# Swapping the halves of the rotated queries: a DMA from SBUF to SBUF in place of a permutation matmul

## The reference

```
q = rope((h @ w_q + b_q).reshape(bsz, s, N_Q_HEADS, HEAD_DIM), pos)
...
sc = jnp.einsum('bnqkgd,bnskd->bnkgqs', q, k_band,
                preferred_element_type=jnp.float32) * (HEAD_DIM ** -0.5)
```

```
t1, t2 = tf[..., :half], tf[..., half:]
out = jnp.concatenate([t1 * cos - t2 * sin, t2 * cos + t1 * sin], axis=-1)
```

## Time and profile before

| | us |
|---|---|
| median of 3 runs | 1259.94 |
| lowest and highest | 1259.32, 1260.23 |
| the profiled execution, its own time | 1257.77 |
| the profiled execution, span | 1256.0 |
| PE busy | 1228.9 (98% of the span) |
| DVE busy | 310.2 (25%) |
| ACT busy | 200.7 (16%) |
| POOL busy | 45.1 (4%) |
| granted TensorE clock, mean | 0.996 of full speed |

### The profile page before, as it was taken

How to read it: one execution, slowest core, us unless ns; L and a number is a source line. 1 busy time by engine, 2 the same in 40 slices (tenths; PEclk the granted TensorE clock), 3 DMA queues, 4 the chain that set the end, 5 groups by cost and what they waited for, 6 DMA issues and landing times.

```text
span 1256.0 us, 29092 instructions
## 1 busy us (share of the span) xinstructions
PE 1228.9 (98%) x13809; PEld 676.1 (54%) x13809; DVE 310.2 (25%) x408; ACT 200.7 (16%) x279; POOL 45.1 (4%) x41
## 2 busy tenths in 40 slices
PE   7999999989999999999999999999999999999996
PEld 6888888879743363355336335533633553363343
DVE  4554545468450101011010101101010110001002
ACT  4444443465420000000000000000000000000001
POOL 3000000011010000000000000000000000000000
PEclk9999999999999999999999999999999999999998
DMA  9965655323489999999999999999999999999960
GB/s 345 391 241 183 200 174 196 134 67 124 157 325 386 402 415 402 396 412 406 405 400 416 398 400 411 411 401 396 411 407 397 412 412 399 399 414 403 386 263 36
DMA packets 97757, 418.72 MB, mean 333 GB/s; under 512 B 8545, under 2 KB 14738, under 8 KB 97634
## 3 DMA queue, kind: packets, MB, share of 16 engines
q1 hardware_dynamic: 94288, 410.59, 83.6%
q0 software_dynamic: 1664, 5.05, 1.4%
q10 hardware_dynamic: 1682, 1.17, 0.3%
HBM read 414.68 MB, written 2.10 MB: 332 GB/s over the span
## 4 chain that ended last, share of the span: by engine, by line
PE 97%; DVE 2%; ACT 1%; DMA 0%; issue 0%; ACTq 0%; DVEq 0%
PE psum L706 46%; PE psum L717 23%; PE psum L618 8%; PE psum L620 7%; PE psum L619 7%; PE psum L697 1%; PE psum L626 1%; PE psum L687 0%; DMA consts<-in_table 0%; PE psum L873 0%; PE psum L792 0%; PE psum L896 0%; DVE x_res L1446 0%; PE psum L883 0%; PE psum L994 0%
## 5 line engine op out<-in xcount | busy, mean ns | idle before, releaser
L706 PE MATMUL psum<-up,xg 128*32 128x448 f32 x6144 | 580.4, 539 | 0.6 <-DVE xg L1670 0.6
L706 PEld LDWEIGHTS psum<-up,xg 128*32 128x32 f32 x6144 | 198.8, 110 | 373.3 <-issue 370.1
L717 PE MATMUL psum<-down,hid_t 128*32 128x256 f32 x5376 | 291.5, 379 | 0.0
L717 PEld LDWEIGHTS psum<-down,hid_t 128*32 128x32 f32 x5376 | 174.7, 110 | 117.9 <-issue 3.9
L1419 DVE TENSOR_TENSOR sil<-sil,psum 128x1344 f32<-128x1344 f32 x16 | 24.9, 1554 | 463.9 <-PE psum L706 463.9
L1297 DVE TENSOR_TENSOR low<-raw,high 128x2048 fp32r<-128x2048 f32 x50 | 114.5, 2292 | 79.8 <-ACT high L1031 79.6
L1031 ACT ACTIVATE high<-raw 128x2048 fp32r<-128x2048 f32 x51 | 97.9, 1920 | 82.5 <-PE psum L620 81.7
L618 PE MATMUL psum<-high,a_hi 128*128 128x512 f32 x224 | 87.3, 390 | 0.9 <-DVE a_lo L1334 0.9
L1097 ACT ACTIVATE sil<-psum 128x1344 f32<-128x1344 f32 x16 | 20.7, 1291 | 421.4 <-PE psum L706 421.4
L620 PE MATMUL psum<-low,a_hi 128*128 128x512 f32 x224 | 87.2, 389 | 0.0
L619 PE MATMUL psum<-high,a_lo 128*128 128x512 f32 x224 | 87.2, 389 | 0.0
(11 more groups left out here) (203 smaller groups left out, 645.5 us busy)
## 6 DMA issues: line engine op xcount, KB each, us to landing
up<-in_moe_w SPq DMA_DIRECT2D x256, 896.0 KB, 8.1
down<-in_moe_w SPq DMA_DIRECT2D x112, 1024.0 KB, 8.2
raw<-in_ffn_w SPq DMA_DIRECT2D x42, 1024.0 KB, 5.8
raw<-in_w_q SPq DMA_DIRECT2D x4, 1024.0 KB, 5.1
raw<-in_w_o SPq DMA_DIRECT2D x4, 1024.0 KB, 4.9
x_res<-in_x SPq DMA_DIRECT2D x2, 512.0 KB, 4.9
raw<-in_pool_w SPq DMA_DIRECT2D x1, 1024.0 KB, 10.3
raw<-in_w_kv SPq DMA_DIRECT2D x1, 1024.0 KB, 5.4
```

The lines of the kernel that those rows point to most:

```text
L706: mm = pe.matmul(out3[g * BLK:(g + 1) * BLK, r, :], xg[:, k, r * BLK:(r + 1) * BLK], w[:, g], start=k == 0, stop=k == DT - 1)
L717: mm = pe.matmul(Y[g * BLK:(g + 1) * BLK, r, :], hid_t[:, c, r, b * BLK:(b + 1) * BLK], w[:, bb, g * GW:(g + 1) * GW], start=c == 0 and b ...
```

## The change

The four `permute` matmuls are taken out. In their place ACT, right behind `add_bias(m+1)`, waits for `biased` and `roped` and issues four DMAs, each of 32 partitions by 512 numbers (64 KB), from `rope_x` to the other half's place in `rope_z`; the four make one swapped tile of 256 KB and raise `swapped` by 16 each. DVE's `rotate(m)` waits for all four and multiplies `rope_z` by the sine in place. The keys are still permuted on PE.

```diff
-            def permute(m):
-
-
-                pe.wait_ge(biased, m + 2)
-                pe.wait_ge(roped, m + 1)
-                pe.matmul(banks[Q_TURNED][:], perm, rope_x[:, (m + 1) % 2].rearrange("p a t -> p (a t)"),
-                          start=True, stop=True).then_inc(permuted, 1)
...
+            def swap_halves(m):
+
+
+                half_d = HD // 2
+                act.wait_ge(biased, m + 2)
+                act.wait_ge(roped, m + 1)
+                for r in range(0, P, half_d):
+                    to = r ^ half_d
+                    act.dma_start(rope_z[to:to + half_d], rope_x[r:r + half_d, (m + 1) % 2]).then_inc(swapped, 16)
...
             add_bias(1)
+            swap_halves(0)
             split(U_Q + 3)
             add_bias(2)
+            swap_halves(1)
             split(U_O)
             exponentials(0, 0)
             exponentials(0, 1)
             add_bias(3)
+            swap_halves(2)
             take_probs(0, 0)
...
             add_bias(4)
+            swap_halves(3)
             take_attended(0)
             split(U_O + 2)
             take_probs(1, 0)
...
-                dve.wait_ge(permuted, m + 2)
-                step(dve.tensor_tensor(rope_z[:], bank3(Q_TURNED), both(sin), ALU.mult))
+                dve.wait_ge(swapped, 64 * (m + 1))
+                step(dve.tensor_tensor(rope_z[:], rope_z[:], both(sin), ALU.mult))
```

More of the change, by code:

```diff
@@ L354, in trunk_program @@
         biased, permuted, cosined, roped = sem("biased"), sem("permuted"), sem("cosined"), sem("roped")
+        swapped = sem("swapped")
         scored, max_ready, exped = sem("scored"), sem("max_ready"), sem("exped")
@@ L926, in _ @@
             queries(1, 0)
-            permute(0)
             queries(1, 1)
@@ L930, in _ @@
             queries(2, 0)
-            permute(1)
             queries(2, 1)
@@ L935, in _ @@
             queries(3, 0)
-            permute(2)
             turn_probs(0, 1)
@@ L942, in _ @@
             scores(2)
-            permute(3)
             attend(1)
```

## The result

| | before | after |
|---|---|---|
| median of the runs | 1259.63 us (1257.96 to 1260.23) | 1271.17 us (1269.06 to 1272.06) |
| profiled execution | 1257.77 us, span 1256.0 | 1272.06 us, span 1270.2 |
| granted TensorE clock, mean | 0.996 | 0.988 |

The changed kernel takes 1.0088 times as long [1.0073, 1.0103]: 11 us slower. The forecast was 1261.0, in a range up to 1264.8.

A forecast was written before the change was run, and what follows sets the result against it. PE was taken as the bound. Place by place: first rotation +1.1, first turn +0.9, level after `permute(2)`'s 0.86, last rotation +1.1; sum +1.1 on the median 1259.94 gives 1261.0 us, range 1259.2 to 1264.8.

The forecast's parts named there:

- What bounds the kernel: PE, busy 879.7 of 891 us from 365 us on; a shift in the attention stage reaches the end one to one.
- What is removed: Four permutations of 0.86 us on PE; only `permute(2)` lies on the path, the first two and last are worth nothing.
- The price of an issue: Each of sixteen DMAs on ACT's queue takes 0.40 us, so each swap holds ACT 1.6 us.
- Rival B: Issuing costs more: at 0.6 us a DMA ACT is held 2.4 us each time, +2.3 us, 1262.2; chance 0.06.
- Place 2: DVE's work from first rotation to first turn: it carries +1.0 on, hiding ACT's rounding, late by +0.8; the turn goes +0.9.
- the signs of being wrong: Wrong altogether if the experts' stage changes its length, or if ACT waits long for `roped` ahead of the issues.
- The landing: Time from a swap's last issue to its tile being there: 2.8 us, and 3.4 us for the last swap.
- My lower end: Lowest landing taken for a swap: 2.0 us, from a 3.0 us row less about 1.0 for its bytes.
- 3.4 us for the last swap: Landing ahead of the last rotation, issued by 314.0 and landed 317.4, where two loads and a 512 KB row take 5.5 and 5.6.
- Rival A: Swaps wait behind the weight loads and land like a load, at the first and last rotation: +4.9 us, 1264.8; chance 0.20.
- about 2L - 4.5: The sum of the change for a landing of L us, counted nearly twice; it passes 2.5 us at L = 3.5.
- What would show it: Signs: issues of 0.3 to 0.45 us, first `rotate` at about 293.4, first projection at about 318.8.

The follow-up runs named there:

- e14: The changed kernel with only the second and third swap by DMA, issued by SP ahead of the weight load, the others PE matmuls: 1258.35 us, ratio 0.9988.
- e1: The kernel before, permutations kept on PE, plus sixteen DMAs issued by ACT to memory that nobody waits for: 1264.44 us, ratio 1.0036.
- e9: The changed kernel with POOL's gain load moved behind the last rotation and SP's two weight loads held until the last swap landed: 1267.89 us, ratio 1.0058.
- e15: The changed kernel with SP issuing each swap ahead of its weight load, two late loads held, gain's load later, spare PE matmuls: 1260.73 us, ratio 1.0004.
- e2: The changed kernel with the four DMAs of each swap issued by SP behind the weight load, instead of by ACT: 1266.63 us, ratio 1.0056.
- e5: The changed kernel with one DMA of 128 partitions a swap in place of four, each half landing in its own place: 1264.34 us, ratio 1.0043.
- e6: The changed kernel with 6, 12, 14 and 6 spare matmuls ahead of PE's four longer waits: 1267.70 us, ratio 1.0061.
- e13: The kernel before, permutations kept on PE, plus sixteen DMAs issued by ACT from SBUF to SBUF, with no wait for a swapped tile: 1268.24 us, ratio 1.0064.
- e7: The changed kernel with only the second and third swap by DMA, issued by SP behind the weight load, the others PE matmuls: 1259.84 us, ratio 0.9997.

## Why the prediction was wrong

1. **What bounds the kernel** held. The experts' stage has 879.57 busy of 891 us, as in the earlier trace rows, and every shift of the attention stage reached the end.
2. **What is removed** held for the two that e14 takes off: `permute(1)` is worth about nothing, as the first turn starts at 302.61 where it was 302.73, and with `permute(2)` the stage is 0.9 us shorter. That the first and the last are worth nothing was not tested by itself.
3. **The price of an issue**, the 0.40 us "a piece", failed: 0.64 us from start to start (the issue itself 514 to 740 ns), outside the bounds of 0.28 and 0.48. The nearest rows were DMAs from memory; this one, from SBUF to SBUF, costs more. Rival B had 0.6 us and a chance of 0.06 for want of such a row, and priced it at +2.3 us.
4. **Place 2, "hidden under +1.0"**, failed with it. The first rotation came 2.0 us later than before, where I had +1.1, and so ACT, which waits for it ahead of the second swap, stood 0.7 us (its bias ended at 296.74, the first issue began at 297.48). The sum had no such wait, though it stood among the signs of being wrong. ACT's rounding was not hidden: DVE's split waited 0.92 us for it, the second rotation came 4.26 - 1.65 = 2.6 us later than before, and the collision with POOL made +3.4 at the first turn where I had +0.9. Even at 0.44 us an issue, near my price, e1 costs 4.6 us without any wait for a landing. PE's waits there, 1.7 and 2.0 us, less the 0.7 that it waited before, are 3.0 of it; the other 1.6 are by estimate the clock (0.79 in 307 to 315 us). The forecast set the permutations' time against the hold, and so it seemed small.
5. **The landing.** The "2.8 us behind the last issue" was right for the first swap, 295.88 - 292.94 = 2.9. By the Trainium skill's fit, cited there, 2.15 (the section states it for a DMA issued by GpSimd); a swap with nothing ahead of it lands in 2.0 (e9, e15), so for a lone one the trace agrees. My lower end, 3.0 us less "about 1.0 for its bytes", would have been 1.7 at the 400 GB/s that I used beside it. The "3.4 us for the last swap" failed: 6.0. Rival A's mechanism came true in full there and only there, at 0.20 for both places; its sum, "about 2L - 4.5", is 2L - 5.1 by my own steps, so its threshold was 3.8 us and not 3.5. The rule that I had set against it, engines taking turns between queues, I had read as letting the swap pass most of the load; in the change none of its packets moved for 3.7 us. The same section of the Trainium skill (DMA: Bandwidth & Descriptors, Queues, rings and completion order) also says that the increment of the semaphore is a write that lands only after every earlier write of that DMA engine, across its queues. The order of the landings fits it: 2.0 to 2.8 us ahead of a load (e14, e15), 2.6 to 3.9 behind one, 5.6 to 6.3 behind two. But it can't be most of the delay: the tile landed 0.4 us behind 327.40, when the last packet had moved, and the 3.7 us lie before the first. Here the data waited.
6. **Rivals A and B together** were never priced. With 0.64 us an issue and 6.0 us for the last landing, my own steps give about +6: B's +2.3 and the 2.6 us more of landing make +4.9, the hold of 0.64 in place of 0.6 us an issue 0.3, and ACT's wait of 0.7 us for the first rotation the rest. That is near the 6.0 which the trace shows outside the stretches at the lower clock.
7. **The clock** was not in the sum. I took PE's waits as the whole cost of being late. Behind waits of 3.2 to 3.6 us the granted clock fell to the lower level and PE's work of the next 8 us or so took half as long again or more: 6.6 us, half of the loss. Nor was the collision of POOL and DVE, 0.8 us.
8. **What would show it**: the sign "issues above 0.5 us B, landings above 3.5 us A" pointed right on both, the second at the last swap alone (6.0; the first had 2.9); the first projection, looked for at about 318.8, came at 329.33.

What stays open: why the clock dips at 267 to 271 us in ten of the profiles, why the clock falls to 0.57 behind one wait and to 0.79 behind the same wait in another profile, and why an issue from SBUF costs more to SBUF than to memory.

## What to carry to other kernels

Count a DMA that a computing engine issues as work of that engine (here, for 64 KB out of SBUF, 0.44 us to memory and 0.64 to SBUF), and ask what stands behind it; issue it from an idle queue, and ahead of the bulk load of that moment, not behind it: here its data waited for the load's, though that was on another queue. A matmul that is moved off PE saves only what PE didn't wait for anyway: move those whose result is wanted late, and keep the others. When PE is the bound, price a new wait of some 3 us with the slower clock behind it, here, in the profile of the change, about as much again.

## What the runs showed of the hardware that was not expected

- A DMA of 64 KB from SBUF to SBUF holds its issuing engine 0.64 us from start to start, on ACT and on SP alike (2.5 us for four, e2); into memory 0.44 (e1); one of 256 KB over 128 partitions 0.47 to 0.53 (e5).
- Its landing was 2.0 to 2.8 us ahead of an 896 KB load, 2.6 to 3.9 us behind one (3.3 where the load was issued 0.9 us before it, 2.8 where 1.5), 5.6 to 6.3 us behind two. These are medians of the four pieces of a swap. Behind two, its packets did not move for 3.7 us.
- The granted clock fell behind single waits of PE of 3.2 to 3.6 us (0.50 to 0.81 in stretches of 4 us after), of 2.2 and 2.5 (e6 0.60, e13 0.63), and behind one of 1.7 us in e1 (0.79 in 307 to 315) and of 1.6 in e2 (0.82 in 300 to 307). It did not behind one of 2.0 in e1, of 1.6 ahead of `scores(0)` in the change and of 1.4 in e7 (1.00 each); behind one of 2.7 us it fell in ten profiles of 17, and not in the others.
- Products on POOL and DVE at the same time: 3.34 us in place of 1.30 on POOL, 1.51 in place of 0.69 on DVE, each when it came second.
